# Two float32r result parts and earlier one-hot rows in a mixture-of-experts combine

## What is computed

```python
scores = sigmoid(x @ w_router)                     # 256 tokens, 64 experts
combine = weights of the 6 chosen experts, 0 elsewhere
hid = silu(x @ w_gate[e]) * (x @ w_up[e])          # per expert e
routed = sum over e of (hid * combine[:, e]) @ w_down[e]
```

## Time and profile before

| what | value |
|---|---|
| median of 3 runs | 1755.2 us (1754.45 to 1755.74) |
| span of the profiled execution | 1752.8 us |
| difference of the two | 2.4 us |
| PE busy | 1607.8 us, 92% |
| VectorE busy | 518.0 us, 30% |
| ScalarE busy | 698.3 us, 40% |
| DMA | 510.50 MB, mean 291 GB/s |

### The profile page before, as it was taken

The page is one execution under the profiler, slowest core; times in us unless marked ns, Lnnn a source line. Parts: engine busy times, 40 slices in busy tenths (PEclk is TensorE's granted clock), DMA queues, the critical chain, the costliest instruction groups (busy, mean ns, idle before and its releaser), DMA issues.

```text
span 1752.8 us, 30448 instructions
## 1 busy us (share of the span) xinstructions
PE 1607.8 (92%) x13039; PEld 1131.2 (65%) x13039; DVE 518.0 (30%) x857; ACT 698.3 (40%) x1055; POOL 18.6 (1%) x25
## 2 busy tenths in 40 slices
PE   5999999989999999999997998999999999999995
PEld 3767766856666666666665776866666666666663
DVE  1034044151222223232323216232222223232324
ACT  2213322233454545454544204225454545454444
POOL 0000000010000000000000000010000000000000
PEclk8999888989999999999998999899999999999998
DMA  9967566546999999999998333438999999999970
GB/s 315 323 227 266 193 251 240 204 168 272 354 370 357 366 358 365 359 358 367 354 370 301 87 118 156 186 126 320 356 368 359 354 365 363 364 358 366 353 286 25
DMA packets 130113, 510.50 MB, mean 291 GB/s; under 512 B 11257, under 2 KB 19601, under 8 KB 97297
## 3 DMA queue, kind: packets, MB, share of 16 engines
q1 hardware_dynamic: 124832, 506.23, 75.9%
q10 hardware_dynamic: 5232, 3.57, 0.7%
HBM read 506.64 MB, written 3.15 MB: 291 GB/s over the span
## 4 chain that ended last, share of the span: by engine, by line
PE 58%; ACT 23%; DVE 12%; issue 5%; DMA 1%; DVEq 1%; ACTq 0%
PE psum L1230 57%; ACT arena L503 22%; DVE arena L1121 8%; DVE arena L1032 1%; PE psum L1551 1%; DMA arena<-in_moe_router_bias 1%; DVE arena L803 0%; DVE arena L1126 0%; ACT arena L526 0%; DVE arena L845 0%; ACTq L500 0%; DVEq L1134 0%; ACT arena L744 0%; ACT L514 0%; PE psum L1698 0%
## 5 line engine op out<-in xcount | busy, mean ns | idle before, releaser
L1230 PE MATMUL psum<-arena 128*64 128x256 f32 (+9 forms) x12756 | 1577.3, 348 | 112.9 <-DVE arena L1032 63.7
L1230 PEld LDWEIGHTS psum<-arena 128*64 128x64 f32 (+3 forms) x12756 | 1100.9, 136 | 582.4 <-issue 347.1
L503 ACT ACTIVATE arena<-psum 128x512 f32<-128x512 f32 (+4 forms) x514 | 455.7, 903 | 573.8 <-PE psum L1230 468.0
L1121 DVE TENSOR_TENSOR arena<-psum,arena 128x512 f32<-128x512 f32 x128 | 137.7, 1076 | 523.8 <-ACT arena L503 523.8
L503 ACT ACTIVATE arena<-arena 128x512 bf16<-128x512 f32 (+1 forms) x144 | 88.6, 625 | 148.8 <-DVE arena L1121 146.2
L1126 DVE TENSOR_TENSOR arena<-arena 128x512 bf16<-128x512 f32 x128 | 88.7, 693 | 101.1 <-ACT arena L503 101.1
L1105 DVE COPY arena<-psum 128x512 f32<-128x512 f32 x64 | 44.3, 693 | 182.4 <-PE psum L1230 182.4
L825 DVE TENSOR_TENSOR arena<-psum,arena 128x16 f32<-128x16 f32 x12 | 2.1, 175 | 144.4 <-PE psum L1230 144.4
L510 ACT ACTIVATE arena<-arena 128x512 f32<-128x512 f32 x20 | 12.3, 629 | 73.6 <-DVE arena L845 73.6
L845 DVE SCALAR_TENSOR_TENSOR arena<-psum,arena 128x128 f32<-128x128 f32 x64 | 17.8, 343 | 65.6 <-PE psum L1230 65.6
L676 ACT ACTIVATE arena<-psum 128x256 f32<-128x256 f32 x64 | 24.7, 386 | 30.0 <-PE psum L1230 30.0
(11 more groups left out here) (137 smaller groups left out, 309.6 us busy)
## 6 DMA issues: line engine op xcount, KB each, us to landing
arena<-in_moe_w_gate SPq DMA_DIRECT2D x64, 2048.0 KB, 7.9
arena<-in_moe_w_up SPq DMA_DIRECT2D x64, 2048.0 KB, 12.6
arena<-in_moe_w_down SPq DMA_DIRECT2D x64, 2048.0 KB, 9.3
arena<-in_ada_w SPq DMA_DIRECT2D x24, 2048.0 KB, 15.1
arena<-in_hgrn_w_in SPq DMA_DIRECT2D x10, 2048.0 KB, 13.5
arena<-in_na_w_qkv SPq DMA_DIRECT2D x6, 2048.0 KB, 18.1
arena<-in_hgrn_w_out SPq DMA_DIRECT2D x1, 4096.0 KB, 12.6
arena<-in_na_w_o SPq DMA_DIRECT2D x1, 4096.0 KB, 13.7
```

What stands on the lines that cost most here:

```text
L503: return act.activation(out, in_, ACT.Copy, **kw)
L1121: dve.tensor_tensor(y_rest[:, :, ps].rearrange("s k p -> s p k"), psum[:, 6 + half, :].rearrange("s (p k) -> s p k", k=K), y[:, j, 0, :, p ...
L1230: return pe.matmul(out, lhsT, rhs, start=start, stop=stop, skip_group_check=True, **kw)
```

## The change

The result parts go from three bf16 parts to two float32r parts. `y` and the transposed one-hot rows `onehot_t` become tensors of type float32r of their own, placed at fixed addresses inside the arena; `route` and the shared expert's intermediates share the room of `y`. Part 0 is ScalarE's copy of PSUM into float32r, part 1 is VectorE's subtract, written straight into float32r. `y_rest`, the middle copy on ScalarE and the low-part subtract on VectorE go. The combine takes 16 matmuls per pair where it took 24. `y_low` and `y_mid` go; the combine waits for `y_rest`.

The one-hot rows of pair n+2 are built in VectorE's step of pair n, behind hid and the gather copy, into the buffer that pair n has finished with; before, the rows of pair n+1 were built at the head of that step. The rows of the second pair are built ahead of the loop.

```diff
-        onehot_t = sc(2 * P, (2, 2, P), BF16)
-        y = sc(3 * D, (2, 3, K, P), BF16)
-        route = sc(12 * 2 * E, (12, 2, E))
+        y_at = sc.room(2 * 2 * D)
+        y = rounded("results", 2 * 2 * D, (2, 2, K, P), y_at)
+        onehot_t = rounded("slots_to_tokens", 2 * 2 * P, (2, 2, P), sc.room(2 * 2 * P))
+        route = cut(12 * 2 * E, (12, 2, E), at=y_at + 2 * D)
...
+        def rounded(name, n, shape, at):
+            names = "abcd"[:len(shape)]
+            v = nc.alloc_sbuf_tensor_at(name, [P, n], F32R, offset=base + 4 * at)[:, :]
+            return v.rearrange(f"p ({' '.join(names)}) -> p {' '.join(names)}", **dict(zip(names, shape)))
...
 # ScalarE, pair_step
                     copy(y[:, j, 0, :, half * (P // 2):(half + 1) * (P // 2)].rearrange("s k p -> s p k"),
                          psum[:, 6 + half, :].rearrange("s (p k) -> s p k", k=K)).then_inc(M.y_high, 1)
-                    ps = slice(half * (P // 2), (half + 1) * (P // 2))
-                    act.wait_ge(M.y_rest, n * 2 + (half + 3))
-                    copy(y[:, j, 1, :, ps], y_rest[:, :, ps]).then_inc(M.y_mid, 1)
...
-            def pair_step(M, r, n, j, next_expert):
-                if next_expert is not None:
-                    one_hots(M, r, next_expert, 1 - j)
+            def pair_step(M, r, n, j, after_next, last=False):
                 dve.wait_ge(M.silu, n + 1)
                 dve.wait_ge(M.hot_t, n + 1)
                 dve.scalar_tensor_tensor(out=hid[:, j], in0=silu[:, j], scalar=slot_w[:, j:j + 1],
                                          in1=psum[:, 4, F:2 * F], op0=ALU.mult, op1=ALU.mult).then_inc(M.hid, 1)
-                if next_expert is not None:
+                if not last:
                     gathered(M, n + 1, 1 - j)
+                if after_next is not None:
+                    one_hots(M, r, after_next, j)
                 for half in range(2):
                     dve.wait_ge(M.y_high, n * 2 + (half + 1))
                     ps = slice(half * (P // 2), (half + 1) * (P // 2))
-                    dve.tensor_tensor(y_rest[:, :, ps].rearrange("s k p -> s p k"),
+                    dve.tensor_tensor(y[:, j, 1, :, ps].rearrange("s k p -> s p k"),
                                       psum[:, 6 + half, :].rearrange("s (p k) -> s p k", k=K),
-                                      y[:, j, 0, :, ps].rearrange("s k p -> s p k"), ALU.subtract).then_inc(M.y_rest, 1)
-                    dve.wait_ge(M.y_rest, n * 2 + (half + 3))
-                    dve.wait_ge(M.y_mid, n * 2 + (half + 1))
-                    ins = dve.tensor_tensor(y[:, j, 2, :, ps], y_rest[:, :, ps], y[:, j, 1, :, ps], ALU.subtract)
-                ins.then_inc(M.y_low, 1)
+                                      y[:, j, 0, :, ps].bitcast(F32).rearrange("s k p -> s p k"), ALU.subtract)\
+                       .then_inc(M.y_rest, 1)
...
 # VectorE, experts_pass
+                one_hots(M, r, 2, 1)
                 gathered(M, r * PAIRS, 0)
-                pair_step(M, r, r * PAIRS, 0, 2)
-                with dve.Fori(0, PAIRS // 2 - 1) as h:
+                pair_step(M, r, r * PAIRS, 0, 4)
+                with dve.Fori(0, PAIRS // 2 - 2) as h:
                     for i in (1, 2):
-                        pair_step(M, r, r * PAIRS + h * 2 + i, i % 2, h * 4 + 2 * (i + 1))
-                pair_step(M, r, r * PAIRS + PAIRS - 1, 1, None)
+                        pair_step(M, r, r * PAIRS + h * 2 + i, i % 2, h * 4 + 2 * (i + 2))
+                pair_step(M, r, r * PAIRS + PAIRS - 3, 1, E - 2)
+                pair_step(M, r, r * PAIRS + PAIRS - 2, 0, None)
+                pair_step(M, r, r * PAIRS + PAIRS - 1, 1, None, last=True)
...
 # PE, combine and down
-                    for part in range(3):
+                    for part in range(2):
                         ins = mm(psum[:, k // 2, (k % 2) * NT:(k % 2 + 1) * NT], y[:, j, part, k],
                                  onehot_t[:, j].rearrange("p a t -> p (a t)"), False, False)
...
-                    pe.wait_ge(M.y_low, n)
+                    pe.wait_ge(M.y_rest, n * 2 + 2)
                     combine(M, 1 - j)
```

More of the change, by code:

```diff
@@ L24 @@
 BF16 = mybir.dt.bfloat16
+F32R = mybir.dt.float32r
 I32 = mybir.dt.int32
@@ L80, in build @@
         arena = ctx.enter_context(nc.sbuf_tensor("arena", [P, WORDS], F32))
+        base = nc.sbuf_base - 4 * WORDS
         top = [0]
+        def rounded(name, n, shape, at):
+            names = "abcd"[:len(shape)]
+            v = nc.alloc_sbuf_tensor_at(name, [P, n], F32R, offset=base + 4 * at)[:, :]
+            return v.rearrange(f"p ({' '.join(names)}) -> p {' '.join(names)}", **dict(zip(names, shape)))
         def cut(n, shape=None, at=None, dtype=None):
@@ L133, in __init__, with room @@
                 self.at, self.end = at, at + size
+            def room(self, n):
+                self.at += -self.at % 8 + n
+                assert self.at <= self.end, (self.at, self.end)
+                return self.at - n
             def __call__(self, n, shape=None, dtype=None):
@@ L157, in build @@
         h_rest = xg
-        y_rest = route.rearrange("p n a e -> p (n a e)")[:, 0:D].rearrange("p (k t) -> p k t", k=K)
         sq = cut(K * NT, (K, NT), at=scratch_at)
-        sh_room = y[:, 0].rearrange("p i k t -> p (i k t)").bitcast(F32).rearrange("p (n a f) -> p n a f", n=3, a=2)
+        sh_room = cut(3 * 2 * F, (3, 2, F), at=y_at)
         sh_silu, sh_hid, sh_hidT = (sh_room[:, n] for n in range(3))
@@ L270, in __init__ @@
                 self.y_ps = [s("y_ps0"), s("y_ps1")]
-                self.y_high, self.y_rest, self.y_mid, self.y_low = s("y_high"), s("y_rest"), s("y_mid"), s("y_low")
+                self.y_high, self.y_rest = s("y_high"), s("y_rest")
                 self.done = s("moe_done")
@@ L1601, in experts @@
                         experts_pass(M, r + 1)
-                pe.wait_ge(M.y_low, more * PAIRS + PAIRS)
+                pe.wait_ge(M.y_rest, more * (2 * PAIRS) + (2 * PAIRS + 2))
                 combine(M, 1, last=True)
```

## The result

The changed kernel takes 1631.94 us (median of 4 runs, 1630.01 to 1633.04) against 1754.97 us (4 runs), a ratio of 0.9298 (95% interval 0.9285 to 0.9311): 123.0 us less, where 122.2 were forecast. The runs agree to 0.2%.

The account below looks back on a forecast made before the run. PE work plus one stall per pair was taken to bound the loop. Stall 63.7, combine 45.9 and layer ends 12.6 us sum to 122.2 us, taking the 1755.2 us median to 1633 us; range 1618 to 1680 us.

Parts of the forecast that it names:

- The bound: In the 64-pair loop, PE work plus one stall per pair sets the time; a pair takes 17.41 us.
- The stall: PE's wait before each gather for the one-hot rows: building them a pair earlier removes all 63.7 us.
- The cover: Behind the down product, the second half's subtract frees the PSUM bank 0.86 us before PE is free.
- the rival where the wait stays: Hid or the PSUM bank holds the gather instead; only combine and layer ends gain: 1697 us, chance 0.04 including in-between results.
- The combine: On PE per pair, 16 float32r matmuls at 0.117 us replace 24 bf16 ones: 0.74 us less, 45.9 us in all.
- The low-end bound: For the combine, float32r at the bf16 rate of 0.109 us per matmul would gain 53.9 us.
- The ends: At both layers' ends, PE's earlier start and the quicker last combine save 6.3 us each, 12.6 together; lower bound 7.
- DMA: Rival: weight loads at 386 GB/s hold a pair at 16.3 us, 1674 us, chance 0.20; held at 363 GB/s, 1743 us, 0.03.
- the dips: DMA's share of 0.31 in the 1.07 us before a gather, where nothing is queued; earlier issue closes it.
- The float32 rivals: Combine matmuls cost one float32 record, 0.242 us: 1757 us, chance 0.06; or two, 0.484 us: about 2003 us, chance 0.06.
- The sum: Over the whole kernel, 63.7 + 45.9 + 12.6 = 122.2 us less, giving 1633 us.

Follow-up runs that it names:

- the one-hot rows alone: Kernel before the change with its three bf16 parts kept, only the one-hot rows built two pairs ahead: 1687.49 us, ratio 0.9614.
- The parts alone: Changed kernel with two float32r parts, but the one-hot rows built in their old place at the head of VectorE's step: 1631.74 us, ratio 0.9300.
- the early read alone: Changed kernel with PE reading the number of extra passes ahead of the pass, the branch staying behind the last pair: 1630.77 us, ratio 0.9313.
- the last version: Changed kernel with slots' weights turned by the matmuls that turn the one-hot rows, and PE's read of extra passes early: 1627.01 us, ratio 0.9284.

## Why the prediction was right

**The bound.** "PE work plus one stall per pair sets the time" held: with the stall gone PE is busy 450 of 450 us.

**The stall** was booked at 63.7 us and is worth 60 x 1.13 = 68 (the one-hot rows alone gave 67.5). The cover named for it, the second subtract 0.86 us ahead of PE, was enough in the run with the old copies; in the full change it is 4.6.

**What the working missed** is a second cure in the same change. It booked the sum on the earlier one-hot rows, which do remove the stall by themselves, and never asked what the float32r parts do to the wait; the combine and the ends without the stall stand at 1697 us, in the rival where the wait stays. The parts alone reach 1631.74. The working had the rows' place in VectorE's queue right but did not follow what stands ahead of them: with the middle copy and the low-part subtract gone and ScalarE's copies at 1.1, the last subtract ends before gate/up does and the rows follow it. One stall can be taken away only once, so the sum holds with either cure.

**The combine** was priced at 0.117 us per matmul, between the transposes' 0.113 and half a float32 record, 0.121; it is 0.123. Of the 1.82 us per pair, the stall has 1.13, so 0.69 is left for the combine where 0.74 stood. That is 43 us for 45.9. The low-end bound (0.109, the bf16 rate) was rightly no more than a bound. The rule of the Trainium skill (FP8 and Floating Point Precision, section TensorE Precision Notes) is that true float32 makes four passes, while reduced-precision float32 is cut to 22 bits. If float32r is the reduced form and makes one pass, which no run here shows, the ratio by that rule would be four, an estimate; the trace comes near it with 0.436 against 0.123, a factor of 3.5, though the records are two against one.

**The ends** were booked at 12.6 us and gave 10.8. ScalarE's strided float32r copy took the 1.06 us that was read from the end of the kernel as 1.1. The read and branch behind the last pair were hidden under the old wait of 7.44 us; the working followed the data and not PE's own instructions, and 1.5 us of these came to light in layer 0. The last combine ran at a granted clock of 0.54 and 0.55 in the windows from 897.07 and from 1606.78, near the lower of the two levels (1.2 and 2.4 GHz), after PE had idled 3.65 and 2.18 us, and took 3.5 us or more instead of the loop's 2.15; the working had priced its first bank by the loop's rate, at 0.65 us, and VectorE's first addition came 1.2 and 1.0 us behind PE's start.

**DMA.** At 386 GB/s the loop would have been held at 16.3 us; the changed kernel drew 403 and the floor is 417. The argument that the dips close when loads are issued earlier fits the loop's share of busy DMA, 0.94 before and 1.00 after. The rule of the Trainium skill (DMA: Bandwidth & Descriptors, section Where 436 GB/s comes from) that HBM binds near 358 GB/s per core, a stack's 716 GB/s shared by two cores, does not agree with this kernel on one core, which held 403 and 417 GB/s for over 400 us; the measurement decides.

**The float32 rivals** fall with one record per matmul; the kernel that takes plain float32 shows what they would have cost, 1945 us instead of the 2003 worked out, for the most part since a record there takes 0.218 and not 0.242 (62 x 32 x 0.024 = 48 us).

**The sum** is closer than its terms. The stall gave 4 us more than was booked, the combine 3 and the ends 2 less, so that 122.2 stands beside 121.2 in the traces and 123.0 in the medians; that they cancel is luck.

## What to carry to other kernels

When a stall hangs on the last item of an engine's queue, follow what stands ahead of it: shortening that chain and moving the item forward are two cures for one stall, and their gains don't add. A busy share of DMA near 1.00 does not show that DMA is the bound; take work off the other engine and see whether a wait for a load appears. When a long wait shrinks, look for the engine's own reads and branches that it had covered.

## What the runs showed of the hardware

- A float32r matmul of 128x128 by 128x256 costs 0.123 us in a stream, a bf16 one 0.109 before the change, a plain float32 one 0.436. A bf16 matmul alternating with a float32r one brings the pair of them to 0.24, no less than two of float32r.
- Writing rows with a stride is much dearer in bf16 than in four bytes, on both engines: 128x512 from PSUM took ScalarE 2.45 us in bf16 and 1.06 in float32r, and VectorE 2.4 to 2.6 us in bf16 and 1.06 in float32r.
- The loads held 417 GB/s over 420 us from one queue, 6.29 MB a pair, while PE worked beside them.
- The read of a register value and a branch on PE made 1.5 us of idle time at the end of layer 0; the same instructions made none at the end of layer 1.
- The clock granted to PE after a short idle time is not the same each time: after 2.77 us the last combine of layer 0 took 2.90 us at a granted clock of 0.71 (the early read alone), after 2.76 us it took 2.17 us at 1.00 (the last version), and after 3.65 us 3.68 us at 0.54 (the full change).
